# RWKV-7 block: the output products of a head pair's four chunks moved into one run behind the last chunk's solution

## The reference, cut to what matters

```python
def step(state, inp):
    r_t, w_t, k_t, v_t, kk_t, a_t = inp
    sa = jnp.einsum('bhij,bhj->bhi', state, -kk_t)
    state = (state * w_t[:, :, None, :]
             + sa[..., None] * (kk_t * a_t)[:, :, None, :]
             + v_t[..., None] * k_t[:, :, None, :])
    y_t = jnp.einsum('bhij,bhj->bhi', state, r_t)
    return state, y_t
```

## Time and profile before

| what | us |
|---|---|
| median of 3 runs | 1838.14 |
| the runs | 1834.91, 1838.14, 1838.63 |
| span of the profiled execution | 1833.9 |
| median less that span | 4.2 |
| TensorE busy in the span | 1766.1 (96%) |
| VectorE busy | 866.7 (47%) |
| ScalarE busy | 744.2 (41%) |

### The profile page before, as it was taken

The page is one execution under the profiler, slowest core; times in us unless marked ns, Lnnn a source line. Parts: engine busy times, 40 slices in busy tenths (PEclk is TensorE's granted clock), DMA queues, the critical chain, the costliest instruction groups (busy, mean ns, idle before and its releaser), DMA issues.

```text
span 1833.9 us, 22481 instructions
## 1 busy us (share of the span) xinstructions
PE 1766.1 (96%) x9524; PEld 1450.5 (79%) x9524; DVE 866.7 (47%) x1238; ACT 744.2 (41%) x1094; POOL 514.4 (28%) x115
## 2 busy tenths in 40 slices
PE   6999998999999999999999999999999999999997
PEld 5897766778788787878888888787768888888886
DVE  2016537898998974451114444507855411123243
ACT  5225455555565543252223222525672432222222
POOL 3442210000000001424444444243334344444442
PEclk8999999999999999999999999999999999999999
DMA  4631222010010015322222322222122222222221
GB/s 164 204 135 49 81 90 66 27 49 27 27 49 24 24 41 190 140 94 99 92 92 95 112 92 92 99 96 70 70 92 92 92 103 93 92 92 100 107 92 70
DMA packets 54664, 161.20 MB, mean 88 GB/s; under 512 B 3327, under 2 KB 30335, under 8 KB 39844
## 3 DMA queue, kind: packets, MB, share of 16 engines
q1 hardware_dynamic: 42476, 135.40, 21.4%
q10 hardware_dynamic: 12088, 24.35, 3.9%
HBM read 153.16 MB, written 10.25 MB: 89 GB/s over the span
## 4 chain that ended last, share of the span: by engine, by line
PE 80%; DVE 9%; issue 5%; ACT 4%; DMA 1%; POOL 1%; ACTq 0%; DVEq 0%
PE ps L589 23%; PE ps L591 22%; PE ps L590 22%; PE ps L1004 2%; PE ps L992 1%; ACT w_hi L1268 1%; DVE x_res L1967 1%; PE ps L1082 1%; PE ps L721 1%; PE ps L921 1%; PE ps L711 1%; POOL w_lo L580 1%; DVE inverse L2204 1%; PE ps L1046 1%; PE ps L1012 1%
## 5 line engine op out<-in xcount | busy, mean ns | idle before, releaser
L580 POOL TENSOR_TENSOR w_lo<-w_raw,w_hi 128x2048 fp32r<-128x2048 f32 x111 | 514.2, 4633 | 1289.4 <-ACT w_hi L1268 1289.1
L589 PE MATMUL ps<-ht_hi,w_hi 128*128 128x512 f32 (+1 forms) x1304 | 522.2, 400 | 13.2 <-POOL w_lo L580 4.5
L591 PE MATMUL ps<-ht_hi,w_lo 128*128 128x512 f32 (+1 forms) x1304 | 497.7, 382 | 0.0
L590 PE MATMUL ps<-ht_lo,w_hi 128*128 128x512 f32 (+1 forms) x1304 | 497.3, 381 | 0.0
L1268 ACT ACTIVATE w_hi<-w_raw 128x2048 fp32r<-128x2048 f32 x126 | 241.3, 1916 | 463.6 <-PE ps L591 405.5
L589 PEld LDWEIGHTS ps<-ht_hi,w_hi 128*128 128x128 f32 x1304 | 247.7, 190 | 71.6 <-issue 23.3
L591 PEld LDWEIGHTS ps<-ht_hi,w_lo 128*128 128x128 f32 x1304 | 247.1, 190 | 48.1
L590 PEld LDWEIGHTS ps<-ht_lo,w_hi 128*128 128x128 f32 x1304 | 248.3, 190 | 39.5 <-issue 1.7
L2420 DVE TENSOR_TENSOR hid_lo<-hidden,hid_hi 128x1024 fp32r<-128x1024 f32 x27 | 129.3, 4788 | 149.1 <-ACT hid_hi L1772 149.1
L589 PE MATMUL ps<-w_hi,hid_hi 128*128 128x512 f32 x432 | 168.2, 389 | 0.0
L591 PE MATMUL ps<-w_hi,hid_lo 128*128 128x512 f32 x432 | 168.1, 389 | 0.0
(11 more groups left out here) (304 smaller groups left out, 2456.2 us busy)
## 6 DMA issues: line engine op xcount, KB each, us to landing
w_raw<-in_wpack SPq DMA_DIRECT2D x114, 1024.0 KB, 4.8
w_raw<-in_wpack SPq DMA_DIRECT2D x24, 512.0 KB, 5.2
bias_skewed_dram<-bias_rows_dram ACTq DMA_DIRECT2D x1, 3840.0 KB, 23.3
toe<-bias_skewed_dram ACTq DMA_DIRECT2D x1, 3072.0 KB, 12.9
x_res<-in_x SPq DMA_DIRECT2D x4, 512.0 KB, 6.0
gate_back<-gate_dram ACTq DMA_DIRECT2D x2, 1024.0 KB, 6.8
gate<-gate_dram ACTq DMA_DIRECT2D x1, 2048.0 KB, 8.4
x_res<-in_x ACTq DMA_DIRECT2D x1, 2048.0 KB, 7.8
```

The costliest lines, as they stand in the source:

```text
L580: nc.gpsimd.tensor_tensor(Wl[:, slot, :], raw[:, slot, :], f32(Wh[:, slot, :]), ALU.subtract).then_inc(lo_ready, 1)
L589: mm(dst, wh, ah, start=first, stop=False)
L590: mm(dst, wh, al, start=False, stop=False)
L591: return mm(dst, wl, ah, start=False, stop=last)
```

## The change

The output products leave `chunk_out`. A new function, `chunk_outs`, stands at the place of chunk 3's `chunk_out` and makes the output products of all four chunks in one run, four products per chunk, first L1056's kind for both heads, then L1057's kind for both. Since all four solutions are now needed at once, ScalarE writes each into its own quarter of ORW's slice of this pair, and `sa_sb` is gone; `raw_out` later overwrites the slice with the outputs. Bank 2 is opened once, by chunk 1's state product, instead of once per chunk. The waits on `gate0_stored` on ScalarE move up, since ORW is now written earlier.

```diff
--- before.py
+++ after.py
@@ -288,7 +288,6 @@
         identR = r("ident_r", [P, P], F32R)
         S = r("state", [P, P])
         RH = r("rhs_sb", [P, P])
-        SA = r("sa_sb", [P, P])
         assert r.at <= y_at + 4 * NT * D
         r = Region(base)
         LW = [place("lora_w0", [P, 2, P], at=x_at + 4 * 3 * 1280)[0], r("lora_w1", [P, 2, P])]
@@ -1036,7 +1035,7 @@
                     last = mm(ps[:, 3, heads(h)], GM[h][:, t, 1, :], TV[:, t, heads(h)], start=t == 0, stop=t == 0 or h == 1)
                 inc(last, "rhs_full")
                 if t:
-                    mm(ps[:, 2, tok(t)], S[:], ra[:, t, 0, :], start=True, stop=False)
+                    mm(ps[:, 2, tok(t)], S[:], ra[:, t, 0, :], start=t == 1, stop=False, skip_group_check=True)
 
             def chunk_solve(a, t):
                 if t == 0:
@@ -1048,15 +1047,21 @@
 
             def chunk_out(a, t):
                 w("sa_ready", NT, a, t + 1)
-                if t < NT - 1:
-                    mm(ps[:, 3, 2 * P:3 * P], TB[:, t, :], SA[:], start=True, stop=False)
-                    last = mm(ps[:, 3, 2 * P:3 * P], TK[:, t, :], TV[:, t, :], start=False, stop=True)
-                    inc(last, "s_full")
-                for h in range(2):
-                    mm(ps[heads(h), 2, tok(t)], TV[:, t, heads(h)], GM[h][:, t, 0, :], start=t == 0, stop=False)
-                    last = mm(ps[heads(h), 2, tok(t)], SA[:, heads(h)], GM[h][:, t, 2, :], start=False, stop=True)
-                if t == NT - 1:
-                    inc(last, "y_full")
+                mm(ps[:, 3, 2 * P:3 * P], TB[:, t, :], ORW[:, a, tok(t)], start=True, stop=False)
+                last = mm(ps[:, 3, 2 * P:3 * P], TK[:, t, :], TV[:, t, :], start=False, stop=True)
+                inc(last, "s_full")
+
+            def chunk_outs(a):
+
+                w("sa_ready", NT, a, NT)
+                for t in range(NT):
+                    for h in range(2):
+                        mm(ps[heads(h), 2, tok(t)], TV[:, t, heads(h)], GM[h][:, t, 0, :], start=False, stop=False,
+                           skip_group_check=True)
+                    for h in range(2):
+                        last = mm(ps[heads(h), 2, tok(t)], ORW[:, a, t * P + HD * h:t * P + HD * h + HD], GM[h][:, t, 2, :],
+                                  start=False, stop=t == NT - 1, skip_group_check=True)
+                inc(last, "y_full")
 
 
             def to_tokens(b, k):
@@ -1133,7 +1138,10 @@
                         key_roots(c)
                     fill()
                     if has_a:
-                        chunk_out(a, t)
+                        if t < NT - 1:
+                            chunk_out(a, t)
+                        else:
+                            chunk_outs(a)
                     fill()
                 if has_b:
                     level_x(b, 4)
@@ -1542,7 +1550,7 @@
 
             def solved(a, t):
                 w("sa_full", NT, a, t + 1)
-                inc(actf(SA[:], ps[:, 3, P:2 * P], ACT.Copy), "sa_ready")
+                inc(actf(ORW[:, a, t * P:(t + 1) * P], ps[:, 3, P:2 * P], ACT.Copy), "sa_ready")
 
             def key_squares(c):
                 act.wait_ge(*half_taken(HALF["rkv", c, 1]))
@@ -1616,6 +1624,9 @@
                     take_half(last)
                 if has_a:
                     rhs(a, 0)
+                    if a == 0:
+                        act.wait_ge(gate0_stored[0], 16 * 4)
+                        act.wait_ge(gate0_stored[1], 16 * 4)
                     solved(a, 0)
                 if gate_last and p < 7:
                     take_half(last)
@@ -1685,8 +1696,6 @@
                     output_squares(a)
                     output_hi(2)
                 if a == 0:
-                    act.wait_ge(gate0_stored[0], 16 * 4)
-                    act.wait_ge(gate0_stored[1], 16 * 4)
                     act.wait_ge(gate_stored, 16 * 2)
                 if has_a and p < 7:
                     raw_out(a)
```

## The result

The changed kernel takes **1851.1 us** (median of 5 runs, 1850.49 to 1855.35), the kernel before in the same session 1838.14 (5 runs, 1834.91 to 1838.63): a ratio of 1.0078, with a 95% interval of 1.0067 to 1.0089. It is slower by 13 us, 0.8%. I had forecast +5.0 us and 1843.1, with a range to 1847.5. The sign is right, the size is not, and the range doesn't hold the time.

The account below looks back on a forecast made before the run. TensorE was taken as nearly full, but feeding and waiting for VectorE. Pairs 0 to 4 (4.45), 5 (0.3), 6 (0.58) and 7 (-0.3) sum to +5.0 us, taking 1838.14 to 1843.1, range 1837.5 to 1847.5.

Parts of the forecast that it names:

- The block in its old place frees 0.74 us, the block in the run costs 0.44: On TensorE, removing a block frees 0.74 us; each added behind chunk 3 costs 0.44, three make the run 1.32 longer.
- Chunk 0 gains 0: At chunk 0, the next products L984 wait for VectorE's L2192, which doesn't depend on the outputs: gain 0.
- Chunk 1 gains 0: At chunk 1 of pairs 0 to 6, L1034 needs VectorE's decayed state, so TensorE's 0.74 us becomes waiting: gain 0.
- Chunk 2 gains 0.45, pair 4 0.35; a full step +0.87: Chunk 2's slack gives 0.45 us, 0.35 in pair 4; against +1.32, pairs 0 to 3 get 0.87 longer each.
- Pair 5 +0.3: In pair 5, with less filler, two waits for VectorE take up part of the 1.32 us: +0.3 (0 to 0.86).
- Pairs 6 and 7, +0.58 and -0.3: Pair 6 gains 0.74 us at chunk 2, net +0.58; pair 7 gains at chunks 0 and 2, net -0.3.
- ScalarE's copies and the earlier waits for the stores: 0: On ScalarE, solution copies go to rwkv_out at equal cost and gate0_stored waits move earlier, stores long issued: 0 us.
- Throughput decides: Rival: TensorE's throughput sets the time; 24 changes of form at 0.30 us go, 7.2 us faster, 1830.9; chance 0.10.
- Absorbed: Rival: later waits for VectorE take up a full step's lateness; 1838.7 us, or 1840.9 if half absorbed; chance 0.28.
- Not side by side: Rival: in the new order the half-width products don't overlap; +1.76 us per pair, 14.1 in all, 1857.2; chance 0.05.

Follow-up runs that it names:

- only1: Against the kernel before, only chunk 1's output products go to the run behind chunk 3; chunks 0 and 2 stay in place: 1839.41 us, ratio 1.0014.
- fill1: Against the kernel before, only chunk 1's output products go to the run and a filler piece of three products moves into their gap: 1836.02 us, ratio 0.9992.
- filled: Changed kernel plus output products made again at their old places, chunk 0 in every pair, chunks 1 and 2 in pair 5: 1843.9 us, 1.0038 of the kernel before.
- keep0: Against the changed kernel, chunk 0's output products stay in place and only those of chunks 1 and 2 move: 1840.49 us, ratio 1.0018 to the kernel before.
- again: The changed kernel measured and traced once more, no edit: 1848.6 us, ratio 1.0061 to the kernel before.
- twice0: Changed kernel with chunk 0's four output products made twice, at their old place and in the run: 1848.19 us, ratio 1.0051 to the kernel before.
- only2: Against the kernel before, only chunk 2's output products go to the run; chunks 0 and 1 stay in place: 1839.65 us, ratio 1.0013.

## Why the prediction was wrong

Point by point, by its steps:

- **The block in its old place frees 0.74 us, the block in the run costs 0.44.** Right. The run got 1.31 us longer (1.32). Where a whole block could be gained, the step got shorter by 0.80 (chunk 2 of pair 6) and 0.79 (chunk 0 of pair 7), so going into and out of the half-width form costs 0.3 to 0.35 us. The rule of the Trainium skill, "TensorEngine Tiling (Array Packing)", Key Properties, on draining at a change of mode agrees with the trace, at 0.30 to 0.35 us, and as the prediction said it decides nothing here.
- **Chunk 0 gains 0.** Right for the path, and this is where the prediction fails. L983 starts 0.06 behind L2201, and waits 0.68.
- **Chunk 1 gains 0: "TensorE comes 0.74 earlier and waits 0.74 longer".** The wait is 0.79, on the path it costs nothing (`only1`, `fill1`).
- **Chunk 2 gains 0.45, pair 4 0.35; a full step +0.87.** Right: -0.47 at chunk 2 of pair 1 and -0.48 at that of pair 3 (from L1051 to L1033), and steps of 0.84 to 0.96 where the clock holds.
- **Pair 5 +0.3.** 0.68, inside its bounds (0 to 0.86). The L991 behind the first wait comes 0.78 us later than in the kernel before (1.32 less that wait and a little more). The second wait got shorter, from 0.93 to 0.46, but its VectorE instruction comes late too, so L991 behind it is still 0.66 later: this wait took 0.12 of the lateness, where I had booked 0.56.
- **Pairs 6 and 7, +0.58 and -0.3.** 0.52 and -0.36.
- **ScalarE's copies and the earlier waits for the stores: 0.** Nothing of them shows in the steps.
- **The rivals.** "Throughput decides" is refuted: all 24 changes of form went, and only those with no wait for VectorE behind them gave their time back. "Absorbed" is refuted: the steps of `filled` each keep their 0.9. "Not side by side" is refuted: 16 steps in 1.8 us.

**The failed step** is the one that priced the new idle time. The prediction reads a granted clock of 1.00 in the earlier trace rows and carries it over to the changed kernel, and books the 0.74 us at chunks 0 and 1 as time that TensorE may just as well wait. It then worked out what the work on the path does, and never what the idle time does to the engine that is idle. With 2.25 of 3.40 us busy in place of 2.84 the clock fell, for 3.4 us each time, and the filler behind it, which is on the path, took nearly twice its time (0.43 us for 0.23). Four such stretches made 6.3 us in the profiled run, three made 4.4 in the second. The trace of before gave reason to name such a fall as a rival, since ahead of the pairs it has a stretch with a lower mean clock, but it could not have given the price: that fall, at 309.4 us, stands behind a wait of 2.89 us, with TensorE busy 0.51 of 3.40 us, and the next one, at 821.4, behind a wait of 1.48 us (1.61 of 3.40): neither place is like chunk 0. The stretch ahead of the pairs, and what stands ahead of each of the two falls:

```profile
300.00:332.00 32.00, 28.09 (x176) 23.17 (x175) 30.13 (x58) 13.55 (x24) 0.00 (x0) 0.95 0.09 33
306.00:309.40 3.40, 0.51 (x5) 0.40 (x5) 3.26 (x8) 2.52 (x5) 0.00 (x0) 1.00 0.00 0
818.00:821.40 3.40, 1.61 (x13) 1.17 (x11) 2.74 (x5) 2.15 (x6) 0.00 (x0) 1.00 0.54 229
```

A second error is in what the base stands for; it moved the forecast by nothing, which is the median plus 5.0 either way. I took the 4.2 us between the profiled span and the median as what lies around a span. In every run with both figures that is 1.7 to 1.9 us. So the profiled execution of before took about 1835.7 us, 2.4 below the median, and that remainder is how far executions of one kernel differ. Between the two profiled executions 3.1 us lie ahead of pair 0's L983 (337.63 and 340.71), where both kernels do the same work; the same window of the changed kernel:

```profile
300.00:332.00 32.00, 28.09 (x164) 23.35 (x163) 27.55 (x52) 12.88 (x23) 0.00 (x0) 0.89 0.01 2
```

From the L983 ahead of this window (293.64 and 295.11) to pair 0's the changed kernel loses 1.6 of the 3.1 us, the rest earlier. `keep0`, which has no falls in the pairs, has such a loss there too (3.7 us of its trace), so it isn't laid to the change. By medians the loss is 13.0 us and 11.5 us in the two sessions: 5.4 of schedule, and the rest by my reading mostly falls.

**Shown**: the schedule costs 5.4 us; a stretch of 3.4 us at the lower level costs 1.3 to 1.6 us; in pairs 1 to 4 there are seven of them in the three traces in which chunk 0's block was moved and nothing stands in its gap, and none in the nine others, the kernel before among them. The least busy 3.4 us around chunk 0 of these pairs have 2.2 us of TensorE with the block moved, and 2.8 with it in place or a stand-in there (2.16 to 2.26 and 2.75 to 2.85). More work without falls is not slower. **Not shown**: what decides between a fall and none. Pair 4 of the changed kernel has 2.42 of 3.40 us busy at its chunk 0 (556.30 in the rows above), and only 2.15 in a stretch that starts 0.9 us earlier, and keeps its clock. In pair 5 `again`, `twice0` and `only2` fall, with chunk 2's block moved in all three; the profiled run of the changed kernel and `keep0`, with it moved as well, don't, and none of the seven traces falls there in which that block stands in its place. Ahead of the fall in `twice0` TensorE was busy 2.73 of 3.40 us, more than the 2.42 of that pair 4, so a busy share alone doesn't tell it. One trace per kernel (two of the changed one) doesn't give how often falls come, nor that they are all of what the medians have beyond the schedule.

## What to carry to other kernels

Work that fills the wait of an engine with a granted clock isn't free to move: look at the granted clock of the whole trace, and if it falls anywhere, price a fall at that place as one of the rivals (here 1.5 us for a pair, more than all that was forecast for its step). The places at which the clock is lower before don't tell how much idle time is safe: in the kernel before it fell behind 0.51 and 1.61 us of work in 3.40, in the changed one behind 2.25 in 3.40. A run with useless work in the new gap tells it. A gap made by such a move is worth something only if other work that is late anyway goes into it. And take the time around a span from runs that list both: the difference between one profiled execution and a median also holds how far executions differ.

## What the runs showed of the hardware

- **TensorE can fall to the lower clock behind short waits.** Ahead of the falls at chunk 0 the timeline shows no long gap. The one before 395.9 us, from the changed kernel:

```profile
392.50 0.66 PE L1045 MATMUL ps<-rhs_sb,tinv_full 128*128 128x64 f32 x4
393.53 0.49 PE L1050 MATMUL ps<-rwkv_out,b_chunk 128*128 128x128 f32 x2 [0.37 <-ACT rwkv_out L1553]
393.85 0.39 PE L1051 MATMUL ps<-v_chunk,k_chunk 128*128 128x128 f32 x2
394.90 0.66 PE L983 MATMUL ps<-ident_r,level 128*128 128x128 f32 x4 [0.66 <-DVE level L2201]
```

  Two waits, 0.37 and 0.66 us, and the clock is at 0.50 one microsecond later. A wait like the first is there in the kernel before too (L1052, up to 0.4 us); the second is new. The Trainium skill, "TensorE: Matmul & The Clock Gate", "A second HAM failure mode: psum-queue depth-cycling", tells of a kernel whose short idle times between groups of products make the clock swing between its two levels. The trace agrees, with these waits; I had read the place only for its path.
- **The lower level came in stretches of 3.4, 6.8 and 10.2 us**: 6.8 at 336 us of three traces, 10.2 in pair 5 of two, 3.4 everywhere else in the pairs. `twice0` lost 4.2 us in one stretch of 10.2 us (4.84 less the 0.63 of `filled`).
- **Two half-width products run side by side even where the program has another one between them.** The kernel before writes its block head by head, L1056 and L1057 of one head and then of the other. The trace has the L1056 of both heads first, their passes 13 to 14 ns apart, and then both L1057 (block of the earlier trace rows):

```profile
515.09 0.45 PE L1056 MATMUL ps<-gram,v_chunk 128*64 128x128 f32 x4
515.36 0.40 PE L1057 MATMUL ps<-gram,sa_sb 128*64 128x128 f32 x4
```
